# Expert weights fetched in rows of 1024 columns, two row tiles at a time, and narrow and wide experts in strict alternation

## The reference, cut to what matters

```python
D_MODEL, SEQ, N_EXPERTS, TOP_K = 1024, 256, 8, 2
D_EXPERT = 7 * D_MODEL // 2          # 3584
...
def swiglu(x, w_gate, w_up, w_down):
    return (jax.nn.silu(x @ w_gate) * (x @ w_up)) @ w_down

def moe_swiglu(x, router, w_gate, w_up, w_down):
    logits = (x @ router).astype(jnp.float32)
    top_vals, top_idx = lax.top_k(logits, TOP_K)
    gates = jax.nn.softmax(top_vals, axis=-1)
    combine = jnp.sum(jax.nn.one_hot(top_idx, N_EXPERTS, dtype=jnp.float32) * gates[..., None], axis=-2)
    y = jnp.zeros_like(x)
    for e in range(N_EXPERTS):
        y = y + combine[..., e:e + 1].astype(x.dtype) * swiglu(x, w_gate[e], w_up[e], w_down[e])
    return y
```

## Time and profile before

| | us |
|---|---|
| median of 3 executions | 1616.21 (1614.83 to 1619.98) |
| the profiled execution, device time | 1619.26 |
| its span in the profile | 1617.5 |
| first expert matmul in the profile | 663.39 |
| last matmul of the combine ends | 1605.85 |

### The profile page before, as it was taken

One profiled execution on the slowest core, in us unless ns is written; L12 is line 12 of the kernel. 1 busy time (PEld: TensorE's weight loads), 2 busy tenths in 40 slices (PEclk: granted clock), 3 DMA queues, 4 the chain that ended last, 5 costly groups with the idle time before them and its releaser, 6 DMA issues.

```text
span 1617.5 us, 22158 instructions
## 1 busy us (share of the span) xinstructions
PE 1541.0 (95%) x7950; PEld 1286.4 (80%) x7950; DVE 1260.5 (78%) x1224; ACT 1041.4 (64%) x972; POOL 126.6 (8%) x148
## 2 busy tenths in 40 slices
PE   9999999999999898999999999998999998999886
PEld 9888988888896797788888888776887776887664
DVE  5687475555647565789889889899898889898988
ACT  5564444443436443678778777887777887778774
POOL 3103010000104201000000000000000000000220
PEclk9999999999999999899999999999999999999988
DMA  9437856465465462799999999999999999999994
GB/s 356 167 131 239 308 176 221 137 219 187 168 210 181 141 211 66 251 385 335 390 388 387 388 379 369 388 387 387 388 387 388 388 387 387 388 387 389 381 381 173
DMA packets 239042, 484.32 MB, mean 299 GB/s; under 512 B 8352, under 2 KB 11456, under 8 KB 238944
## 3 DMA queue, kind: packets, MB, share of 16 engines
q1 hardware_dynamic: 229744, 454.06, 78.1%
q0 software_dynamic: 7440, 25.83, 4.9%
q10 hardware_dynamic: 1760, 3.15, 0.5%
HBM read 477.21 MB, written 14.18 MB: 304 GB/s over the span
## 4 chain that ended last, share of the span: by engine, by line
PE 61%; DVE 14%; DMA 12%; issue 8%; ACT 3%; POOL 1%; SPq 0%; DVEq 0%; ACTq 0%; POOLq 0%
PE bank L427 16%; PE bank L429 16%; PE bank L428 16%; DVE w_lo L2150 4%; DMA raw<-in_moe_w_up_dram 3%; DMA raw<-in_moe_w_down_dram 3%; DMA raw<-in_moe_w_gate_dram 2%; PE bank L417 2%; PE bank L420 2%; PE bank L419 2%; ACT w_hi L1183 2%; DMA c_add<-gate_rows 2%; DVE w_lo L1593 2%; DVE w_lo_more L2150 1%; PE bank L906 1%
## 5 line engine op out<-in xcount | busy, mean ns | idle before, releaser
L1183 ACT ACTIVATE w_hi<-raw 128x2048 fp32r<-128x2048 f32 (+1 forms) x322 | 608.2, 1894 | 236.5 <-PE bank L429 161.6
L2150 DVE TENSOR_TENSOR w_lo<-raw,w_hi 128x2048 fp32r<-128x2048 f32 x221 | 502.3, 2288 | 69.2 <-ACT w_hi L1183 64.8
L1593 DVE TENSOR_TENSOR w_lo<-raw,w_hi 128x2048 fp32r<-128x2048 f32 (+1 forms) x96 | 211.1, 2203 | 144.4 <-ACT w_hi L1183 144.1
L427 PE MATMUL bank<-w_hi,xe_hi 128*128 128x512 f32 x460 | 182.8, 397 | 0.2
L429 PE MATMUL bank<-w_hi,xe_lo 128*128 128x512 f32 x460 | 179.6, 390 | 0.0
L428 PE MATMUL bank<-w_lo,xe_hi 128*128 128x512 f32 x460 | 179.2, 390 | 0.0
L2150 DVE TENSOR_TENSOR w_lo_more<-raw,w_hi_more 128x2048 fp32r<-128x2048 f32 x63 | 144.1, 2288 | 15.0 <-ACT w_hi_more L1183 9.4
L427 PE MATMUL bank<-w_hi,xT_hi 128*128 128x512 f32 (+1 forms) x384 | 146.9, 383 | 0.1
L429 PE MATMUL bank<-w_hi,xT_lo 128*128 128x512 f32 (+1 forms) x384 | 144.5, 376 | 0.0
L428 PE MATMUL bank<-w_lo,xT_hi 128*128 128x512 f32 (+1 forms) x384 | 144.4, 376 | 0.0
L1183 ACT ACTIVATE w_hi_more<-raw 128x2048 fp32r<-128x2048 f32 x64 | 122.8, 1918 | 23.2 <-PE bank L429 7.9
(11 more groups left out here) (356 smaller groups left out, 3023.1 us busy)
## 6 DMA issues: line engine op xcount, KB each, us to landing
raw<-in_moe_w_gate_dram SPq DMA_DIRECT2D x96, 1024.0 KB, 11.3
raw<-in_moe_w_up_dram SPq DMA_DIRECT2D x96, 1024.0 KB, 11.0
raw<-in_moe_w_down_dram SPq DMA_DIRECT2D x96, 1024.0 KB, 11.4
raw<-in_mem_wkv_dram SPq DMA_DIRECT2D x16, 1024.0 KB, 7.4
raw_more<-in_moe_w_up_dram SPq DMA_DIRECT2D x16, 1024.0 KB, 13.5
raw_more<-in_moe_w_gate_dram SPq DMA_DIRECT2D x16, 1024.0 KB, 10.7
raw_more<-in_moe_w_down_dram SPq DMA_DIRECT2D x16, 1024.0 KB, 12.0
raw<-in_c_w_in_dram SPq DMA_DIRECT2D x12, 1024.0 KB, 5.1
```

The source lines that it names most:

```text
L427: nc.tensor.matmul(d, xh, hi[:, k, :], start=(first and k == 0), stop=False)
L1183: return nc.scalar.activation(dst, src, ACT.Copy)
L1593: tt(w_lo[s][:, 0:n], raw[c % NRAW][:, 0:n], w_hi[s][:, 0:n].bitcast(F32), ALU.subtract).then_inc(lo_made, 1)
L2150: tt(w_lo[s][:, :], raw_exp[r][:, :], w_hi[s][:, :].bitcast(F32), ALU.subtract).then_inc(lo_made, 1)
```

## The change

Three things are changed, all in the expert part.

1. **Shape of a chunk.** For the first six of the seven blocks of gate and up, a chunk is now two row tiles by 1024 columns, and its products go into two banks: four chunks of gate for the blocks `j` and `j + 1`, then four of up. The seventh block keeps the old shape. The 14 chunks of down are two row tiles by all 1024 columns, into the banks 4 and 5 together, except in the last job, which keeps two halves. So 38 of a job's 42 chunks have the new shape, and 24 of the last job's. The bytes, the splits and the count of matmuls of a job stay.
2. **The steps around it.** The tables `GATE_END`, `UP_END`, `C_GATE`, `C_UP`, `C_FOLD`, `C_HID` and `C_LOW` place the copy of a gate bank, the product with up and the fold of the blocks; blocks now end in pairs. Both halves of `y` are taken out and sent after chunk 41, where the first was after chunk 34.
3. **The jobs.** `NARROW` is 4, `PAIRS` 3, and so one wide job stands ahead of the pairs: w n w n w n w z where it was w w w n w n w z (z is narrow too).

```diff
-    NARROW, PAIRS = 3, 2
+    NARROW, PAIRS = 4, 3
...
-    ORDER = [0, 1, 4, 2, 5, 3, 6]
+    ORDER = [3, 0, 4, 1, 5, 2, 6]
...
+        DBL = EJ // 2
+        RK = CK // 2
+        GATE_END = [8 * (j // 2) + 3 if j < 2 * DBL else 8 * DBL + 1 for j in range(EJ)]
+        UP_END = [8 * (j // 2) + 7 if j < 2 * DBL else 8 * DBL + 3 for j in range(EJ)]
+        C_GATE = {GATE_END[j] + j % 2: j for j in range(EJ)}
+        C_UP = {UP_END[j] + j % 2: j for j in range(EJ)}
+        C_FOLD = {UP_END[j] + 2 + 2 * (j % 2): j for j in range(EJ)}
...
+                if idx is not None and len(outs) == 2:
+                    both = [w[s][:, :].rearrange("p (k c) -> p k c", k=n) for w in (w_hi, w_lo)]
+                    for k in range(n):
+                        for i, (_, dst) in enumerate(outs):
+                            wh, wl = (w[:, k, i * cols:(i + 1) * cols] for w in both)
...
+                            nc.tensor.matmul(dst[:, :], xh, wh, start=begin, stop=False)
+                            nc.tensor.matmul(dst[:, :], xh, wl, start=False, stop=False)
+                            m = nc.tensor.matmul(dst[:, :], xl, wh, start=False, stop=end)
...
-                    src = w[0][bass.ds(e, 1), k0 * P:(k0 + CK) * P, col:col + W].rearrange(
+                    src = w[0][bass.ds(e, 1), k0 * P:(k0 + n) * P, col:col + CHUNK // n].rearrange(
                         "e (k p) c -> p (e k) c", p=P)
                     s = c % NEXP
-                    sp.dma_start(raw_exp[s][:, :].rearrange("p (k c) -> p k c", k=CK), src)\
+                    sp.dma_start(raw_exp[s][:, :].rearrange("p (k c) -> p k c", k=n), src)\
...
-                    if (c == 4 * EJ + EK // CK - 1 or c == EC - 1) and (last or not narrow):
-                        i = (c - 4 * EJ) // (EK // CK)
+                    for i in range(2):
+                        if c != (EC - 1 if i or not last else C_HALF) or (narrow and not last):
+                            continue
```

More of the change, by code:

```diff
@@ L859, in expert @@
                     idx = N0 + c + EC * job
-                    if c < 2:
-                        pe.wait_ge(emptied[c], start[c] + JOB_CLAIMS[c] * job)
+                    if c == 0:
+                        for b in range(2):
+                            pe.wait_ge(emptied[b], start[b] + JOB_CLAIMS[b] * job)
                     if c == C_INDEX:
@@ L945, in _, with expert_chunks @@
                 sp.dma_start(dst, src).then_inc(raw_in[c % NRAW], 16)
-            def expert_chunks(e, job, first=False):
+            def expert_chunks(e, job, first=False, last=False):
                 for c in range(EC):
@@ L1543, in expert @@
                         turned(f"{z}xB", job)
-                    for at_c, i, of, made in ((C_NARROW_Y, 0, "n", job), (C_WIDE_Y, 1, "w", job - 1)):
-                        if c == at_c and z == of:
-                            act.wait_ge(sem(f"y_made{i}"), made + 1)
-                            act.dma_start(y_rows[i][bass.ds(made * P, HP), :],
+                    if c == C_WIDE_Y and z == "w":
+                        for i in range(2):
+                            act.wait_ge(sem(f"y_made{i}"), job)
+                            act.dma_start(y_rows[i][bass.ds((job - 1) * P, HP), :],
                                           y[0:HP, i * W:(i + 1) * W]).then_inc(sem(f"y_kept{i}"), 16)
@@ L2123, in expert @@
                     idx = N0 + c + EC * job
-                    if not narrow and c < 4 * EJ and c % 4 == 3:
-                        j = c // 4
-                        dve.wait_ge(chunk_used, idx + 1)
+                    if not narrow and c in C_UP:
+                        j = C_UP[c]
+                        dve.wait_ge(chunk_used, N0 + UP_END[j] + EC * job + 1)
                         wait_emptied(dve, f"{z}eg{j}", job)
@@ L2134, in expert @@
                         nc.vector.nop().then_inc(emptied[fillings[f"{z}eu{j}"][0]], 1)
-                    if narrow and not last and (c == 4 * EJ + EK // CK - 1 or c == EC - 1):
-                        i = (c - 4 * EJ) // (EK // CK)
+                    for i in range(2):
+                        if c != EC - 1 or last or not narrow:
+                            continue
                         dve.wait_ge(chunk_used, idx + 1)
@@ L2168, in expert @@
                                    eT_two[:, 4 * j:4 * j + 4, 0:HP].bitcast(F32), ALU.subtract), f"{z}et{j}")
[L2169 to L2170 removed]
+                    if not narrow and c in C_HID:
+                        j = C_HID[c]
                         dve.wait_ge(sem("eT_hi_made"), EJ * job + j + 1)
```

97 lines of the change are left out of this document (63 added, 34 removed).

## The result

The changed kernel takes 1623.91 us (median of 15 runs, 1619.66 to 1626.38), the kernel before 1616.95 (1614.83 to 1620.02). The ratio is 1.0044, with a 95% interval of 1.0035 to 1.0052: slower, by more than the 0.3% that can be told from no change. The forecast was 1586, with a range that ended at 1612. The profiled execution took 1621.89 us (span 1620.2), 32.2 more than the 1589.7 forecast for it.

A forecast was written before the change was run, and what follows sets the result against it. Transfers at 388 GB/s were taken to bind the job pairs, PE the wide jobs ahead. 118.7 + 3 x 223.8 = 790.6 us replaced 817.7; with 2.5 from the last job, -29.6 us gave 1586, range 1575 to 1612.

The forecast's parts named there:

- Step (a): Expert weight transfers: 4 KB rows raise the rate from 388 to 407 GB/s, a chunk costs 2.576 us instead of 2.703.
- rival B: Weight transfers: smaller fixed cost per row, rate 400 GB/s or a little under, pairs still transfer-bound, 1594 us; chance 0.13.
- Step (b): PE and DVE with quicker transfers: a narrow job's floor is 104.6 us, a pair of jobs 222.1.
- Step (d): Paired gate and up blocks, later folds and neighbouring bank copies: cost nothing, except 0.5 us for a later start.
- Its own last part: Signs to check: rate 400 or more with narrow-to-wide marks near 110 us means DVE waits for ACT or its step order.
- Step (c): End of a wide job: ACT sends both halves of `y` before the next split, +1.2 us at each of four ends.
- Step (e): Job order: one more narrow job replaces a PE-bound wide one; the four smallest experts fit 64 tokens, nothing is run again.
- rival C: Weight transfers: rate stays at 388 GB/s, only two PE-bound wide jobs are gained, -3 to -5.5 us, 1612 us; chance 0.13.
- The clock: PE's granted clock: a long fall in the fourth narrow job would upset the sum; left outside it, no size given.
- The one on the slower side: Wide jobs' ends: rate stays, transfers run dry at the boundary and the end shows, +5 us, 1621 us; chance 0.06.
- Those by a lower rate: Weight transfers: rate 400 GB/s or a little under (1594 us, chance 0.13) or still 388 (1612 us, chance 0.13).

The follow-up runs named there:

- the last kernel: Changed kernel with gate and up paired in wide jobs only, 512-column blocks in narrow ones, loop over pairs written out: 1606.54 us, 0.9924 against the kernel before.

## Why the prediction was wrong

- **What bounds the kernel before** was read rightly: with half of its traffic it gains 1.03%. But the forecast asked for more than the engines can give. With all single blocks of gate and up, down paired, the new order of jobs and half of the traffic the time is 1598.03 us, above the 1586; two branches have some 6 us of it.
- **Step (a), the rate: right.** 407 GB/s were forecast, with ends at 400 and 414. The window of 800 to 820 us reads 409, the slices 403 to 412. The Trainium skill, page "DMA: Bandwidth & Descriptors", lists 408.7 for such a stream in its section "iDMA fabric — 4 AXI ports for 8 engines, asymmetric across TPBs": the trace agrees. The 3 cycles a packet in the section "Why small descriptors are slow (HBM only)" of the same page of the Trainium skill, by which the forecast's rival B had 397, are too small a cost here; the measurement decides.
- **Step (b), the floor of the narrow job: right for the old order, 1.2 us low.** 104.6 was forecast and 105.8 measured with half the transfers (105.7 to 106.9 with down paired); 3 x 1.2 = 3.6 us. Of the 5.3 us of waits that it took off as the transfers' doing, 1.4 are a wait between engines. The rest worked, but only for the program it was read in.
- **Step (d), "I cost it at nothing": this is the step that failed.** The order of the folds and copies raises a narrow job from 105.8 to 109.9, 111.5 and 112.1 us, 5.4 on average, 16.1 together (3.6 and 16.1 are the 19.7 missed). The cost is in DVE's waits for ACT's splits, which grow from 1.4 to 5.1, 6.6 and 6.8 us, and in part in PE's clock behind PE's own longer wait. The last job is narrow too, and keeps its down halves: it was to gain 2.5 us and lost 2.4; with single blocks it takes 110.6, and 112.4 with the loop written out, where the changed kernel takes 113.6. The forecast asked only whether each bank and each `eT` was ready for its reader. It did not ask what stands behind a waiting instruction on the same engine. Its own last part named this outcome (a rate over 400, marks near 110, and the order of the steps on ACT as what DVE waits for), but gave it no price and no chance.
- **Not in the sum at all: the branch back.** It happens once more than before, and both are now uncovered: 4.5 us each, 9 us, which is the whole miss on the wide jobs (8.6). It stood in reach: 121.5 against 118.6 between the marks of the kernel before, which was read as transfers, and the branch itself stood in the rows of ACT's order in the section on the change.
- **Step (c), the end of the wide job: right.** 118.7 and 119.2 forecast; 119.0, 119.5, and 118.9 to 119.2 without the loop. Its 1.2 us measured 1.4 to 1.7.
- **Step (e)** held as to what fits a narrow job: the narrow marks are those of narrow jobs in all three. The 3 to 5.5 us that rival C gave to the order of jobs did not show in it alone (0.9998), and only with the loop written out (0.9978).
- **The clock** stood outside the sum, and the forecast said so. It falls in all three narrow jobs, and in two of them it falls behind PE's wait at the last fold, where it costs 1.6 us.
- The first mark came 1.2 us earlier than the sum had it. All together: 0.3 + 19.7 + 8.6 + 4.9 - 1.2 = 32.3, of 32.2.
- **The rivals.** The one on the slower side had nearly the time (1621) but its condition, that the rate stays at 388, is false, and the transfers did not run dry. Those by a lower rate (1594 and 1612) fall with step (a). All of them turned on how fast the transfers run or whether they run dry; the mechanism that came was a new wait between engines. That the slower rival's number is near the measured one is luck.

What stays open: which order of steps would free narrow jobs with paired blocks, since moving two of them left 109.6 us and more, and no run moved the copy or the fold of step 25; and what the pairs would be worth in narrow jobs with an order of steps that doesn't hold ACT. In the last kernel, narrow marks of 109.0 to 111.6 stand against the 105.7 to 106.9 of the engines. Its transfer row above speaks for 2 KB rows and full buffers as the cause, but no run with more buffers was made.

## What to carry to other kernels

Before paying for a faster resource, measure what the others could do with it: one kernel with half of every transfer left out would have shown that some 17 us were to be had, not 30, and, made from the changed program, that its own order had already spent them. An edit of "the steps around it" is to be priced like any other: for each handshake between two in-order engines, count what is queued behind it and how much work the partner holds in hand, above all on the engine that never rests. And where a limit is lifted, list the waits that it hid (here a branch of 4 us and the end of a job), since they come back at full price.

## What the runs showed of the hardware

**The branch back.** ACT's wait behind it is 4.17 us in the changed kernel and 3.58 to 3.89 in the six others with whole transfers and a loop, but 2.11 and 2.26 in the changed kernel with half of the transfers, 2.95 and 3.27 in the one with down alone paired, and 1.45 in the kernel before with half of them. The profile's list of DMA queues has rows of a kind "instruction" beside the weights'; these are the changed kernel's, from 900 to 1280 us, two passes of the loop (packets, MB, share of 16 engines):

```profile
q1 hardware_dynamic: 39658, 141.05, 96.1%
...
q8 instruction: 18, 0.29, 0.3%
```

From 1000 to 1275 us queue q8 has 14 or 15 such packets in the kernels that branch back twice in it, 12 in those that do it once, and 9 or 10 in those without a loop. That the code of the loop's start is fetched again through the same DMA engines, and waits behind the weights, fits all three observations; no run here separates it from another cause.

**TensorE's clock.** Behind PE's wait of 2.87 us the granted clock falls from 1.00 to 0.50, and the matmuls of 512 columns follow each other every 0.43 us instead of every 0.23. It is back at 0.99 from 1100 to 1102 us. With the clock at 1.00 in job 1, the same fold and chunk let ACT go on 1.58 us sooner.

**Row length.** One core's stream of 1 MB transfers runs at 354 GB/s with 1 KB rows (a stretch of 2 us only), 388 with 2 KB and 409 with 4 KB. The line through the first two gave 407.
